# One core, two-layer hybrid decoder: routed expert rows scattered with an add into one row per token, in place of one stored row per assignment

## The reference

```python
def _routed_experts(xf, top_idx, top_w, w_gate, w_up, w_down):
    t, d = xf.shape                    # 512, 1024
    n_assign = t * TOP_K               # 4096 assignments
    ...                                # assignments sorted by expert, in blocks of 128 rows
    def expert_block(args):
        xb, e = args
        return _swiglu(xb, w_gate[e], w_up[e], w_down[e])

    y_rows = lax.map(expert_block, (x_rows, block_e)).reshape(n_rows, d)
    return jax.ops.segment_sum(y_rows * row_w[:, None], row_tok, num_segments=t + 1)[:t]

def _moe(h, ...):
    top_idx, top_w = _route(xf, w_router, router_bias)
    y = _routed_experts(...) + _swiglu(xf, ws_gate, ws_up, ws_down)

for l in range(DEPTH):                 # DEPTH = 2
    ...                                # x = x + gate1 * token_mixer(h)
    x = x + gate2 * _moe(h, ...)
```

## Time and profile before

| | us |
|---|---|
| median of three executions | 2434.42 |
| lowest, highest | 2418.03, 2441.61 |
| span of the profiled execution | 2439.2 |
| TensorE busy in it | 2117.7 (87%) |
| VectorE busy in it | 1845.4 (76%) |
| ScalarE busy in it | 1355.7 (56%) |
| GpSimd busy in it | 454.9 (19%) |

### The profile page before, as it was taken

One profiled execution on the slowest core, in us unless ns is written; L12 is line 12 of the kernel. 1 busy time (PEld: TensorE's weight loads), 2 busy tenths in 40 slices (PEclk: granted clock), 3 DMA queues, 4 the chain that ended last, 5 costly groups with the idle time before them and its releaser, 6 DMA issues. The chain is left out here.

```text
span 2439.2 us, 37993 instructions
## 1 busy us (share of the span) xinstructions
PE 2117.7 (87%) x10096; PEld 1676.7 (69%) x10097; DVE 1845.4 (76%) x2420; ACT 1355.7 (56%) x1724; POOL 454.9 (19%) x345
## 2 busy tenths in 40 slices
PE   2899989999999999994079899889999999999960
PEld 0655577888888888883046457768888878888850
DVE  5636635899999998994773573579899889998957
ACT  2223411677777777772121342157777777777741
POOL 0200300122312222331020011012222222232210
PEclk9987889999999999997569778899999999999985
DMA  7025223799899999994732440279989989899847
GB/s 280 12 82 190 87 85 118 277 349 361 346 339 345 350 351 352 350 353 165 287 128 65 157 137 1 92 268 352 350 330 352 345 327 349 339 352 351 327 160 281
DMA packets 133901, 618.44 MB, mean 254 GB/s; under 512 B 21558, under 2 KB 24630, under 8 KB 80716
## 3 DMA queue, kind: packets, MB, share of 16 engines
q1 hardware_dynamic: 111180, 550.52, 59.9%
q0 software_dynamic: 22656, 67.13, 7.6%
HBM read 581.68 MB, written 43.65 MB: 256 GB/s over the span
## 5 line engine op out<-in xcount | busy, mean ns | idle before, releaser
L1110 POOL DMA_INDIRECT y_rows<-mixT,sidx x136 | 240.0, 1765 | 560.2 <-issue 428.5
L1352 DVE TENSOR_TENSOR w_lod<-raw_d,w_hid 128x2048 fp32r<-128x2048 f32 x136 | 312.6, 2298 | 35.0 <-ACT w_hid L1165 26.0
L1349 DVE TENSOR_TENSOR w_loa<-raw_gu,w_hia 128x2048 fp32r<-128x2048 f32 x136 | 310.2, 2281 | 9.4 <-ACT w_hia L1163 8.9
L1349 DVE TENSOR_TENSOR w_lob<-raw_gu,w_hib 128x2048 fp32r<-128x2048 f32 x136 | 310.2, 2281 | 0.0
L1163 ACT ACTIVATE w_hia<-raw_gu 128x2048 fp32r<-128x2048 f32 x136 | 261.3, 1921 | 26.7 <-PE bank L1507 21.9
L1178 ACT ACTIVATE mixT<-bank 128x512 f32<-128x512 f32 x272 | 147.9, 596 | 209.0 <-PE bank L1507 197.8
L1096 POOL DMA_INDIRECT mixT<-h_rows,gidx x138 | 134.0, 971 | 690.5 <-issue 684.5
L1357 DVE TENSOR_TENSOR hbT_lo<-bank,hbT_hi 128x512 fp32r<-128x512 f32 x272 | 175.2, 686 | 114.6 <-ACT hbT_hi L1171 114.6
L1165 ACT ACTIVATE w_hid<-raw_d 128x2048 fp32r<-128x2048 f32 x136 | 261.1, 1920 | 0.0
L1163 ACT ACTIVATE w_hib<-raw_gu 128x2048 fp32r<-128x2048 f32 x136 | 259.2, 1906 | 0.0
L1505 PE MATMUL bank<-w_hid,actT_hi 128*128 128x512 f32 x544 | 227.3, 418 | 12.7 <-DVE actT_lo L1393 12.7
(11 more groups left out here) (331 smaller groups left out, 3960.3 us busy)
## 6 DMA issues: line engine op xcount, KB each, us to landing
raw_gu<-in_w_gate SPq DMA_DIRECT2D x136, 1024.0 KB
raw_gu<-in_w_up SPq DMA_DIRECT2D x136, 1024.0 KB
raw_d<-in_w_down SPq DMA_DIRECT2D x136, 1024.0 KB
w_ada_sb<-in_w_ada SPq DMA_DIRECT2D x40, 1024.0 KB, 5.7
raw_gu<-y_rows SPq DMA_DIRECT2D x32, 1024.0 KB, 6.5
w_in_sb<-in_w_out SPq DMA_DIRECT2D x16, 512.0 KB, 7.2
w_in_sb<-in_w_in SPq DMA_DIRECT2D x2, 3072.0 KB, 21.8
hT<-in_w_ada SPq DMA_DIRECT2D x4, 1024.0 KB, 11.6
```

The source lines that it names most:

```text
L1110: by_rows(s, lambda rows: pool.indirect_dma_start(out=y_dram, in_=yb[s.par][0:rows], in_offset=None, out_offset=bass.IndirectOffsetOnAxis( ...
L1349: dve.tensor_tensor(w_lo[k][:].rearrange("p c g f -> p g c f"), raw_gu[s.par][:, :, 4 * k:4 * k + 4, :], w_hi[k][:].bitcast(F32).rearrange ...
L1352: dve.tensor_tensor(w_lo[2][:], raw_d[s.par][:], w_hi[2][:].bitcast(F32), ALU.subtract).then_inc(lo[2], 1)
```

## The change

`y_rows` shrinks from 8 x 512 rows to 512 + 128 rows. It is filled with zeros at the start of each expert block: POOL clears half of `raw_d[1]`, and SP writes it out five times, 512 KB each. The scatter gets an add as its operation (`compute_op`): each 4 KB row of `yb` is added in float32 to its token's row in device memory. The index is now the token (column 0 of `listed`) and, for a row that holds no token, row 512 + k, so no entry is out of bounds any more; all entries of one scatter differ. At the end SP reads four tiles of 512 KB, all at once into four buffers, and DVE does two operations for each: times the gate, and plus `x`.

```diff
@@ constants
+    put("spare", T + k)
@@ experts
-        y_part = [raw_gu[k // 2][:, k % 2].rearrange("p c f -> p (c f)").rearrange("p (k n) -> p k n", k=2) for k in range(4)]
+        y_part = [raw_gu[j // 2][:, j % 2].rearrange("p c f -> p (c f)")[:, 0:D] for j in range(TJ)]
-        y_rows = y_dram.rearrange("(k j p) n -> p k j n", p=P, j=TJ)
+        y_rows = y_dram.rearrange("(j p) n -> p j n", p=P)
@@ SyncE
+                sp.wait_ge(s_empty, 1)
+                for j in range(TJ + 1):
+                    sp.dma_start(y_rows[:, j, :], raw_d[1][:, 0, :]).then_inc(s_emptied, 16)
                 sp.wait_ge(s_table, 1)
...
                 sp.wait_ge(s_started, 1)
+                sp.wait_ge(s_emptied, 16 * (TJ + 1))
                 end = steps(sp, step)
                 sp.wait_ge(s_scattered, end.n)
-                for u in range(4 * TJ):
-                    wait(sp, s_ysum, u - 3)
-                    sp.dma_start(y_part[u % 4], y_rows[:, 2 * (u % 4):2 * (u % 4) + 2, u // 4, :]).then_inc(y_in[u % 4], 16)
+                for j in range(TJ):
+                    sp.dma_start(y_part[j], y_rows[:, j, :]).then_inc(y_in[j], 16)
@@ GpSimd
-                bound_h, bound_y = pool.to_reg(T - 1), pool.to_reg(TOPK * T - 1)
+                bound_h, bound_y = pool.to_reg(T - 1), pool.to_reg(T + P - 1)
+                pool.memset(raw_d[1][:, 0, :], 0.0).then_inc(s_empty, 1)
...
+                pool.wait_ge(s_emptied, 16 * (TJ + 1))
                 def scatter(s):
...
                     by_rows(s, lambda rows: pool.indirect_dma_start(
                         out=y_dram, in_=yb[s.par][0:rows], in_offset=None,
                         out_offset=bass.IndirectOffsetOnAxis(ap=sidx[s.par][0:rows, 0:1].bitcast(U32), axis=0),
-                        bounds_check=bound_y, oob_is_err=False).then_inc(scattered_dma[s.par], 16))
+                        bounds_check=bound_y, compute_op=ALU.add).then_inc(scattered_dma[s.par], 16))
@@ VectorE
-                    dve.tensor_scalar(sidx[s.par][:], listed[:, bass.ds(s.n, 1), 1], NO_SLOT, None, ALU.add).then_inc(s_sidx, 1)
+                    dve.tensor_scalar(sidx[s.par][:], listed[:, bass.ds(s.n, 1), 0], NO_SLOT, cst("spare"), ALU.add, ALU.min).then_inc(s_sidx, 1)
...
                 for j in range(TJ):
-                    for k in range(4):
-                        part = y_part[k]
-                        dve.wait_ge(y_in[k], 16 * (j + 1))
-                        if k == 0:
-                            dve.tensor_tensor(yb[0], part[:, 0], part[:, 1], ALU.add).then_inc(s_ysum, 1)
-                        else:
-                            link(dve.tensor_tensor(yb[0], yb[0], part[:, 0], ALU.add))
-                            dve.tensor_tensor(yb[0], yb[0], part[:, 1], ALU.add).then_inc(s_ysum, 1)
-                        dve.wait_ge(s_ysum, 4 * j + k + 1)
-                    link(dve.tensor_tensor(yb[0], yb[0], mod[:, GATE2, :], ALU.mult))
-                    dve.tensor_tensor(x[:, j, :], x[:, j, :], yb[0], ALU.add).then_inc(s_xout, 1)
+                    dve.wait_ge(y_in[j], 16)
+                    dve.tensor_tensor(y_part[j], y_part[j], mod[:, GATE2, :], ALU.mult).then_inc(s_ysum, 1)
+                    dve.wait_ge(s_ysum, j + 1)
+                    dve.tensor_tensor(x[:, j, :], x[:, j, :], y_part[j], ALU.add).then_inc(s_xout, 1)
                     dve.wait_ge(s_xout, j + 1)
@@ host
-    y_rows = nc.dram_tensor("y_rows", (TOPK * T, D), F32, kind="Internal").ap()
+    y_rows = nc.dram_tensor("y_rows", (T + P, D), F32, kind="Internal").ap()
```

More of the change, by code:

```diff
@@ L999, in experts @@
         s_yout, s_sel, s_gidx, s_sidx, s_gathered, s_scattered = (sem(n) for n in "s_yout s_sel s_gidx s_sidx s_gathered s_scattered".split())
-        y_in = [sem(f"y_in{k}") for k in range(4)]
+        y_in = [sem(f"y_in{j}") for j in range(TJ)]
+        s_empty, s_emptied = sem("s_empty"), sem("s_emptied")
         s_xout = sem("s_xout")
```

## The result

The changed kernel takes 2416.1 us (median of 15 runs, 2394.8 to 2426.3) against 2430.6 us for the kernel before (15 runs, 2418.0 to 2441.6): a ratio of 0.9949 with an interval of 0.9926 to 0.9972. That is 14.5 us faster, about half a per cent, so within the 1% that was called no change. The forecast was 2468, slower. The time is inside its range; the likeliest case is not what happened.

The account below looks back on a forecast made before the run. PE paced the loop, but POOL's chain of scatters, 10.05 of 10.43 us, was taken to decide: 2439.2 - 76.4 (ends) + 107.4 (loops) + 2.7 (last scatters) = 2472.9 profiled, 4.8 above its median, so 2468 us; range 2407 to 2557.

Parts of the forecast that it names:

- The layer ends: Read-back at each layer's end: 13.6 us in place of 51.8, saving 76.4 us over both layers.
- Zeroing: Zero writes of `y_rows` before the expert loop: cost 0, hidden behind routing; about 10 us a layer without that cover.
- Volume of the add: Reading old rows and moving fillers in each scatter: 75.2 more row moves on 16 engines, 0.85 us.
- The landing (d = 1.35 in the loop): d, what the add adds to a scatter's landing: 0.85 us of moves plus 0.5 for read before write; bounds 0 to 3.5.
- the first rival: Hidden: old rows are read while the scatter stands behind the weights, d under 0.4; 2358 us, chance 0.17.
- The sum 134 x (8.05 + 2.0 + d): Both expert loops: 134 steps of mean landing, 2.0 us to the next issue, and d; 1527.6 us, 107.4 more.
- Rival 3: DMA engines become the loop's bound, an added row costing four moves; 12.0 us a step, ACT waiting for weights, 2566 us; chance 0.13.
- The break-even: Where the loops' loss evens out the saving at the layer ends: d = 1.1.
- The pace before: Expert loop before the change: one step in 10.43 us, read from ten loads of gate weights.
- Descriptors (rival 4): POOL's own part of a scatter doubles with a third address per row, 1.7 us more; d = 3.05, 2699 us, chance 0.20.
- What was to show it: Expected signs: ends 13 to 15 us, landing 9.4 (4.7 alone), period over 11, PE's waits over 100, share under 92%.
- The way to be wrong that was named: Scatter landing in the loop: it may shrink as the loop slows, since fewer weights stand before it; size then wrong.

Follow-up runs that it names:

- a_plain: The changed kernel without the add (each scatter overwrites), filler rows still moved; 2372.4 us, ratio 0.9763 to the kernel before.
- g_ends_only: The changed kernel without the add and with filler rows dropped; short read-back and zeroing stay; 2365.0 us, ratio 0.9715 to the kernel before.
- h_volume: The kernel before plus one DMA per step on SP's queue, 80 rows of 4 KB into an unused buffer; 2643.3 us, ratio 1.0859.
- d_two_sums: The changed kernel with two sum tensors for even and odd steps, a scatter issued before the previous is waited for; 2401.5 us, ratio 0.9885.

## Why the prediction was right in part and wrong in sign

- **The layer ends: right.** 76.3 saved, 76.4 predicted; the first tile landed after 3.5 us (1175.55 to 1179.06) for 3.2 taken. In a_plain and g_ends_only it arrives whole, to within the 7 us of the fillers.
- **Zeroing: right**, at nothing. The loops begin at 453.7, as at 453.2 in the earlier trace rows.
- **Volume of the add: right.** Two moves per added row, 0.82 us of all engines per step for 0.85, and 6.8 fillers for 7.5.
- **The landing (d = 1.35 in the loop): wrong, too large.** Over all 136 scatters the mean from issue to POOL's notice is 8.04 us before (the six of the earlier trace rows gave 8.05) and 8.62 after: 0.58, not 1.35. Alone, behind no weights, d is larger than was taken: the kernel's last scatter went from 3.4 us in the earlier trace rows to 5.2.

```profile
2382.87 1.40 POOL L1118 DMA_INDIRECT y_rows<-mixT,sidx  x1 [9.80 <-issue]
...
L1126 POOLq EVENT_SEMAPHORE  x1: 17/17/17, 2388.1 to 2388.1; - x1
```

  So d alone is 1.8, and most of it disappears behind the weights in the loop. This is the mechanism of the first rival. How much of it is the read ahead of the write and how much the second move no run took apart.
- **The sum 134 x (8.05 + 2.0 + d): the step that failed.** It made the mean landing the bound of every step, with d = 1.35 in it where 0.58 was measured. With the measured 0.58 it gives 134 x 10.63 - 1420.2 = 4 us more, and the loops lost 58.7. What it leaves out are three things. The first is the spread. A chain with a cushion is broken by its long landings, and PE doesn't win back what it waited for. In the changed kernel (POOL's scatters with a gather between them; when it is told of the scatters; when it tells PE of the gathered block; PE's turn and products):

```profile
868.44 2.77 POOL L1118 DMA_INDIRECT y_rows<-mixT,sidx  x1 [3.49 <-issue]
874.40 0.93 POOL L1102 DMA_INDIRECT mixT<-h_rows,gidx  x1 [3.19 <-issue]
882.86 2.36 POOL L1118 DMA_INDIRECT y_rows<-mixT,sidx  x1 [7.53 <-issue]
...
L1126 POOLq EVENT_SEMAPHORE  x2: 17/17/17, 866.4 to 880.9; - x2
...
L1110 POOLq EVENT_SEMAPHORE  x1: 17/17/17, 883.5 to 883.5; - x1
...
883.53 1.97 PE L1502 MATMUL bank<-const,mixT 128*128 128x128 f32 x8 [1.88 <-POOLq L1110]
...
885.73 0.63 PE L1507 MATMUL bank<-w_lod,actT_hi 128*128 128x512 f32 x1
886.15 0.63 PE L1508 MATMUL bank<-w_hid,actT_lo 128*128 128x512 f32 x1
...
887.48 0.40 PE L1506 MATMUL bank<-w_hid,actT_hi 128*128 128x512 f32 x1
887.72 0.40 PE L1507 MATMUL bank<-w_lod,actT_hi 128*128 128x512 f32 x1
...
884.00:886.00 2.00, 2.00 (x10) 1.90 (x9) 0.49 (x3) 0.46 (x1) 1.23 (x2) 0.50 1.03 430
888.00:890.00 2.00, 2.00 (x11) 1.70 (x10) 2.00 (x1) 0.84 (x2) 0.00 (x0) 1.00 0.83 244
```

  A scatter issued at 868.44 is seen landed at 880.9, 12.5 us later, the longest of all; the next follows 2.0 us behind, as the prediction's model has it, the notice comes at 883.5, 1.8 us after the gather had landed (874.40 and 7.3 us), and PE has stood idle for 1.88 us. The second is the gather, which the prediction never priced. The longest stall of this loop is of that kind:

```profile
826.75 1.00 POOL L1102 DMA_INDIRECT mixT<-h_rows,gidx  x1 [0.68 <-issue]
...
L1110 POOLq EVENT_SEMAPHORE  x2: 17/17/17, 822.8 to 837.8; - x2
...
837.85 1.55 PE L1502 MATMUL bank<-const,mixT 128*128 128x128 f32 x6 [3.95 <-POOLq L1110]
```

  This gather took 11.0 us and the notice went out as it landed. Behind its lateness stand the DMA engines: at 0.97 their lack of room was 0.27 of the 0.44 us, with the gathers as what comes late. The third is PE's own pace. After the stall above the granted clock is 0.50 (the 1.2 GHz level), and the products start 0.42 us apart; at 1.00 they start 0.24 us apart. In the loops this makes 23.8 of the 58.7 us: a stall cost more than its length. Rival 3 named the DMA engines and then put them aside ("10.45, no more than now"), since a mean of 10.45 within a period of 10.43 looked like a tie. It also named the wrong waiter: ACT's waits for weights are 54.6 us in h_volume, none in the changed kernel and at most 7.1 us in the others (d_two_sums).
- **The two errors have opposite signs.** 107.4 was forecast for the loops and 58.7 came. Of the 2472.9 - 2417.6 = 55.3 us by which the profiled execution was missed, 48.7 are the loops, 7.6 the rest where nothing was changed, and the last scatters take back 0.9. The break-even was at 76 us of loss, and "slower" hung on it.
- **The pace before.** 10.43 us was read from ten steps; over all 134 it is 10.60, so some steps already ran late, and the earlier trace rows said so. The model had no term for them.
- **Descriptors (rival 4): a small part is there.** POOL's own part grew by 0.3 us at the first layer's median and 0.5 at the second's, for a bound of 1.7.
- **What was to show it.** Ends of 13 to 15 us: yes. Period over 11 us: just (11.04). The landing of 9.4 in the loop: no (8.62); 4.7 alone: 5.2. PE's waits over 100 us: no, 51.5. PE's share under 92%: no, 569.17 / 590 = 96.5%. The way to be wrong that was named, that the landing shrinks as the loop slows, fits a smaller d; the runs don't separate it from a read that is hidden.
- **The page of the skill.** The Trainium skill, "DMA: Bandwidth & Descriptors", section "Anatomy of one DMA", would make a scatter of 60 rows (246 KB) 2.0 + 0.56 = 2.6 us, an estimate from that page. The traces show 3.4 alone and a mean of 8.04 in the loop, plain; the measurement decides. Its section "Issuing engines are not separate DMA queues" says that all DMAs end up interleaved on the same 16 engines whoever starts them; h_volume agrees, where rows on SP's queue took POOL's gathers from 4.80 to 8.37 us.

What stays open: why a plain row holds an engine longer in h_volume; how d splits; and whether the room that was lacking is the DMA engines' own or the memory's. The loops' 58.7 us are accounted for, by PE's waits for the notice (51.5 - 15.1 = 36.4) and its slower matmuls (23.8).

## What to carry to other kernels

Before you price a longer DMA by its mean landing, look at the spread of the landings and at the busy share of the DMA engines: at 92% there was no room for 0.8 us a step, at 82% the same add, unchained, cost 0.05 us. Price a stall of TensorE above its length: here 36.4 us more of waits came with 23.8 us of slower matmuls. If adds to one place must be serial, two accumulators taken in turn break the chain for the price of one more addition at the end, here 6 us a layer for 0.23 us in each of 67 steps. Drop rows that carry nothing instead of sending them to a spare row (7 to 9 us here, by medians whose intervals overlap).

## What the runs showed of the hardware

- A 4 KB row that is added in an indirect DMA holds a DMA engine for 0.36 us, a plain one for 0.18.
- The same scatter lands 1.8 us later alone (5.2 for 3.4 us) and 0.58 us later on average among the weights.
- A higher busy share need not be more bytes: 350 GB/s at 0.92 and 0.93, 323 at 0.97 with 80 more plain rows a step in h_volume, where a plain row of the indirect queue held an engine for 0.227 us. With adds it is 337 to 341 at 0.97, but there the bytes count each added row once.
- After stalls of PE in the loops the granted clock falls to 0.50. Over the loops it is 0.99 before, 0.97 after and 0.93 in h_volume, and the same 7100 matmuls are busy for 1378.3, 1402.0 and 1456.0 us.
- A gather on POOL's queue gets slower as others send more: medians of 4.80, 5.47, 6.28 and 8.37 us in before, after, d_two_sums and h_volume.
